# State-space input projection: two weight units that split the contraction instead of the columns, 192 matmuls of 512 moving columns for 384 of 256

## The chip, the cores and the metric

The kernel runs on 1 core of one Trainium2 chip. The metric is the device time of the whole kernel in microseconds (us). TensorE (PE) multiplies, VectorE (DVE), ScalarE (ACT) and GpSimd (POOL) work element by element, and SyncE (SP) issues most of the loads. PEld in the profile is TensorE's weight load, which is recorded apart from the matmul.

## The reference

One layer of a hybrid encoder on 1024 tokens of 1024 channels in float32. The part that matters here is the input projection and what becomes of its columns `u`:

```python
h = rmsnorm(x, g_mix_pre[l])
z = h @ w_in[l]                                   # 1024 x 1024 by 1024 x 4864
q, k, v, u, qx, gates = jnp.split(z, _IN_SPLITS, axis=-1)
y_attn = sliding_window_attention(q, k, v, sinks[l])
y_ssm = s5_branch(u, ...)                         # u: 1024 tokens x 512 columns
y_mem = memory_cross_attention(qx, km, vm)
gt = jax.nn.sigmoid(gates.reshape(B, L, N_BRANCH, D_MODEL))
merged = gt[:, :, 0] * (y_attn @ w_branch_attn[l]) + gt[:, :, 1] * (y_ssm @ w_branch_ssm[l]) + gt[:, :, 2] * (y_mem @ w_branch_mem[l])
x = x + rmsnorm(merged @ w_out[l], g_mix_post[l])
# then the MLP: x = x + rmsnorm(square(relu(rmsnorm(x) @ w_up)) @ w_down)
```

The change touches `u` = h times columns 768 to 1279 of `w_in`: 1024 tokens, a contraction of 1024, 512 columns out.

## The kernel before, in words

**Products.** Every large product is made in three matmuls for each 128 rows of the contraction. A float32 operand is split into a rounded part (`hi`) and the rest (`lo`), both of type fp32r, and `product` (L1345) adds hi*hi, hi*lo and lo*hi in a PSUM bank. The first operand of `matmul` after the bank is the stationary one, which a weight load (LDWEIGHTS) puts into the array, and the second is the moving one. Both may be 128 partitions; the moving one has up to 512 columns here. In the rows of the profile, `bank<-whi,hThi` names the moving operand first and the stationary one second.

**Weight units.** The weights come in units of 128 partitions by 2048 elements (1 MB), in two slots of `raw`, `whi` and `wlo`; unit `u` uses slot `u % 2`. For each unit SP issues two DMAs into `raw` (`load`, L293), ACT makes `whi` from it (`prep_hi`, L279), DVE makes `wlo` (`prep_lo`, L285), and TensorE waits for `wlo` (`unit`, L1354). `load` of unit u waits until DVE has made `wlo` of unit u-2. `prep_hi` of unit u waits, through the bank that its last argument names, until TensorE has finished with unit u-2. The units around the change are 9 (gate piece 0), 10 and 11 (`U_U`, the projection of u), 12 (gate piece 1) and 13 (gate piece 2).

**Order.** Each engine has its own order written out by hand, with semaphores between them. The results in PSUM are numbered events; event n uses bank n % 8. TensorE waits with `wait_free` until the bank's event n-8 was taken, and the engine that takes event n waits with `wait_full`. TensorE's order around the change is: gate piece 0 (`g0`, 4 events), scores of the sliding-window attention (`ssc`, 16 events, L1483), projection of u (`u`, 8 events), gate piece 1 (`g1`, 4 events), transposes and products of the attention (`spv`, L1364 and L1524), gate piece 2, and then the state-space layer.

**Projection of u.** `hThi` and `hTlo` hold the normalised input with channels in partitions, 128 channels by 1024 tokens for each of 8 values of k. The state-space layer wants tokens grouped by their number modulo 8, so the stationary operand is a view of `hThi` with step 8: the 128 tokens t = 8c + i for one i, whose elements lie 32 bytes apart in each partition (L1488, `STEP` = 8). Everywhere else in the kernel the stationary operand is contiguous. The moving operand is 256 columns of the weights, so a unit holds all 8 values of k for half of the columns. Two values of i share a bank.

**Other engines meanwhile.** DVE normalises the 16 score tiles (`s_normalise`, L1052 to L1062) while TensorE is in the projection; in DVE's order this stands between `prep_lo` of unit 11 and `prep_lo` of unit 12, and `prep_lo` of unit 13 follows. ACT takes the eight events of u (`copy_out`, L519) and writes them to `uc`, a view of `tok`, for the state-space layer.

Of the kernel before, what the change touches and what calls it, by code (L numbers as in the profile page):

```python
# [19 lines left out]
KT = D // P  # L20
# [5 lines left out]
W512 = 512  # L26
BT = W512 // P
# [3 lines left out]
STEP = 8  # L31
NC8 = L // STEP
NPAIR = 16
SG = 16
ST = 64
RP = 4
C_V, C_U, C_QX, C_G = 640, 768, 1280, 1792
# [3 lines left out]
U_MEM, U_QX, U_Q, U_KV, U_U, U_MERGE_A, U_GLU, U_MERGE_M, U_MERGE_S, U_OUT, U_MLP = 0, 4, 6, 8, 10, 23, 25, 27, 29, 31, 35  # L41
# [9 lines left out]
FIRST = {}  # L51
# [45 lines left out]
def hybrid_layer(nc, a, out):  # L97
# [4 lines left out]
    with ctx:  # L102
# [97 lines left out]
        uc = tok[:, :].rearrange("p (g i c) -> p g i c", g=32, i=STEP)  # L200
# [9 lines left out]
        banks = [ctx.enter_context(nc.psum_tensor(f"bank{b}", [P, 512], f32)) for b in range(8)]  # L210
        bank_full = [sem(f"bank_full{b}") for b in range(8)]
# [40 lines left out]
        def wait_free(eng, n, it=0, per=0):  # L252

            if n >= 8:
                eng.wait_ge(bank_free[n % 8], n // 8 + it * (per // 8))
# [17 lines left out]
        def prep_hi(act, u, n_before, it=0, per=0, ev=0):  # L273

            dmas = 2 * (u // 2 + 1) + (2 if u >= U_Q else 0)
            act.wait_ge(w_loaded[u % 2], 16 * dmas + it * (16 * per))
            if n_before is not None:
                wait_full(act, n_before, it, ev)
            nc.scalar.activation(parts(u)[0], raw[:, u % 2, :], ACT.Copy).then_inc(w_hi, 1)  # L279
# [7 lines left out]
        def wviews(u, kt):  # L287
            w = UNIT // kt
            return (whi[:, u % 2, :].rearrange("p (k c) -> p k c", c=w), wlo[:, u % 2, :].rearrange("p (k c) -> p k c", c=w))


        @block.sync
        def _(sp):  # L293
            def load(u, pieces, it=0, per=0):

                if u >= 2:
                    sp.wait_ge(w_lo, u - 1 + it * per)
                for dst, src in pieces:
                    sp.dma_start(dst, src).then_inc(w_loaded[u % 2], 16)

            def cols(u, src, kt=KT):

                v = raw[:, u % 2, :].rearrange("p (k c) -> p k c", k=kt)
                s = src.rearrange("(k p) c -> p k c", p=P)
                h = kt // 2
                return [(v[:, 0:h, :], s[:, 0:h, :]), (v[:, h:kt, :], s[:, h:kt, :])]

            for idx in range(2):
                sp.dma_start(xst[:, idx, :], a["mem"][0][idx * P:(idx + 1) * P, :]).then_inc(mem_in[idx], 16)
            sp.dma_start(gmem[:, :], a["g_mem"][0].partition_broadcast(P)).then_inc(gains_in, 16)  # L310
            w_in = a["w_in"][0]
            for s in range(4):
                load(U_MEM + s, cols(U_MEM + s, a["w_mem_kv"][0][:, s * 256:(s + 1) * 256]))
            for s in range(2):
                load(U_QX + s, cols(U_QX + s, w_in[:, C_QX + s * 256:C_QX + (s + 1) * 256]))
            for s in range(2):

                u = U_Q + s
                v = raw[:, u % 2, :].rearrange("p (k i j c) -> p k i j c", k=KT, i=2, j=2)
                src = w_in[:, 0:512].rearrange("(k p) (j i c) -> p k i j c", p=P, j=2, c=HD)  # L320
                load(u, [(v[:, :, i, j, :], src[:, :, 2 * s + i, j, :]) for i in range(2) for j in range(2)])
            load(U_KV, cols(U_KV, w_in[:, 512:768]))
            gate = lambda i: load(U_GATE[i], cols(U_GATE[i], w_in[:, C_G + 256 * i:C_G + 256 * (i + 1)]))
            gate(0)
            for s in range(2):
                load(U_U + s, cols(U_U + s, w_in[:, C_U + s * 256:C_U + (s + 1) * 256]))
            for i in range(1, 12):
                gate(i)
            for s in range(2):
                u = U_MERGE_A + s  # L330
                v = raw[:, u % 2, :].rearrange("p (k c) -> p k c", k=BT)
                load(u, [(v[64 * j:64 * j + 64, :, :], a["w_branch_attn"][0][256 * j:256 * j + 256, s * 512:s * 512 + 512]
                          .rearrange("(k p) c -> p k c", p=HD)) for j in range(2)])
            for s in range(2):
                u = U_GLU + s
                v = raw[:, u % 2, :].rearrange("p (k h c) -> p k h c", k=BT, h=2)
                src = a["w_glu"][0].rearrange("(k p) (h c) -> p k h c", p=P, h=2)
                load(u, [(v[:, :, h, :], src[:, :, h, s * 256:(s + 1) * 256]) for h in range(2)])
            for first, name in ((U_MERGE_M, "w_branch_mem"), (U_MERGE_S, "w_branch_ssm")):
                for s in range(2):  # L340
                    load(first + s, cols(first + s, a[name][0][:, s * 512:s * 512 + 512], BT))
            for s, c in enumerate((1, 0, 2, 3)):
                load(U_OUT + s, cols(U_OUT + s, a["w_out"][0][:, c * 256:(c + 1) * 256]))
            up, down = a["w_up"][0], a["w_down"][0]
            with sp.Fori(0, 8) as it:
                for s in range(2):
                    load(U_MLP + s, cols(U_MLP + s, up[:, bass.ds(it * 512 + s * 256, 256)]), it, 4)
                for s in range(2):
                    load(U_MLP + 2 + s, cols(U_MLP + 2 + s, down[bass.ds(it * 512, 512), s * 512:(s + 1) * 512], BT), it, 4)
            for t in range(NT):  # L350
                sp.wait_ge(out_made, t + 1)
                sp.dma_start(out[0, t * P:(t + 1) * P, :], tok[:, (1 + t % 3) * D:(2 + t % 3) * D]).then_inc(out_sent[t % 3], 16)
            for s, count in enumerate((3, 3, 2)):
                sp.wait_ge(out_sent[s], 16 * count)
# [158 lines left out]
        def _(act):  # L513
            A = nc.scalar

            def copy_out(n, dst, src=None):

                wait_full(act, n)
                A.activation(dst, banks[n % 8][:, :] if src is None else src, ACT.Copy).then_inc(bank_free[n % 8], 1)  # L519
# [32 lines left out]
            for s in range(4):  # L552
                n0 = FIRST["front"] + 4 + 6 * s
# [14 lines left out]
            n = FIRST["spar"]  # L568
            copy_out(n, spar[:, :, :].rearrange("p a b -> p (a b)"), banks[n % 8][:, 0:48])

            for s in range(2):
                n0 = FIRST["qx"] + 4 * s
# [18 lines left out]
            for s in range(2):  # L591
                n0 = FIRST["q"] + 4 * s
                prep_hi(act, U_Q + s + 1, n0 - 1)
                for i in range(2):
                    for half in range(2):
                        n = n0 + 2 * i + half
                        copy_out(n, qwin[:, s, i, 8 * half:8 * half + 8, :], banks[n % 8][:, :].rearrange("p (n c) -> p n c", c=CH))
            n0 = FIRST["kv"]
# [35 lines left out]
                    A.activation(prob[:, e, :], prob[:, e, :], ACT.Exp).then_inc(s_exp, 1)  # L634
            A.activation(sinkx[:, :, :], sinkx[:, :, :], ACT.Exp).then_inc(sink_exp, 1)

            for s in range(2):
                n0 = FIRST["u"] + 4 * s
                prep_hi(act, U_U + s + 1, n0 - 1)
                for jj in range(4):  # L640
                    n = n0 + jj
                    src = banks[n % 8][:, :].rearrange("p (j g c) -> p j g c", j=2, c=SG)
                    copy_out(n, uc[:, 16 * s:16 * s + 16, 2 * jj:2 * jj + 2, :].rearrange("p g j c -> p j g c"), src)
            gates(1)

            for q in range(8):
                for nn in range(2):
                    n = FIRST["spv"] + pv_event(q, nn)
# [4 lines left out]
            for ri in range(2):  # L653
                n = FIRST["spc"] + ri
                wait_full(act, n)
                src = banks[n % 8][:, :].rearrange("p (k g o) -> p g k o", g=2, o=SG)
                A.activation(cpk[0:64, ri, :, :], src[0:64, 0, :, :], ACT.Copy)
                A.activation(cpk[64:P, ri, :, :], src[64:P, 1, :, :], ACT.Copy).then_inc(bank_free[n % 8], 1)
            for r in range(4):
                n0 = FIRST[f"s5a{r}"]  # L660
# [5 lines left out]
                for e in range(2):  # L666
                    n = FIRST[f"s5m{r}"] + e
# [25 lines left out]
            for e in range(8):  # L693
                n = FIRST["yg"] + e
# [647 lines left out]
        def _(pe):  # L1342
            T = nc.tensor

            def product(dst, lhs, rhs, kt, start=True, stop=True, ready=None):  # L1345

                for k in range(kt):
                    if ready:
                        ready(k)
                    for i, (p, q) in enumerate(((0, 0), (0, 1), (1, 0))):  # L1350
                        ins = T.matmul(dst, lhs(k)[p], rhs(k)[q], start=start and k == 0 and i == 0,  # L1351
                                       stop=stop and k == kt - 1 and i == 2)
                return ins
# [121 lines left out]
            for e in range(16):  # L1475
                n = FIRST["ssc"] + e
                j = e % 2
# [10 lines left out]
            for s in range(2):  # L1488
                u = U_U + s
                unit(u)  # L1490
                hi, lo = wviews(u, KT)
                for jj in range(4):
                    n = FIRST["u"] + 4 * s + jj
                    wait_free(pe, n)
                    for ii in range(2):
                        i = 2 * jj + ii
                        ins = product(banks[n % 8][:, ii * 256:ii * 256 + 256], lambda k: (hs[0][:, k, i, :], hs[1][:, k, i, :]),
                                      lambda k: (hi[:, k, :], lo[:, k, :]), KT)
                    ins.then_inc(bank_full[n % 8], 1)
            gates(1)  # L1500

            pe.wait_ge(s_prob, 16)
# [228 lines left out]
```

## Time and profile before

| what | value |
|---|---|
| time, median of 3 runs | 1685.59 us (1683.85 to 1686.29) |
| span of the profiled execution, first to last instruction | 1684.2 us |
| PE busy | 1626.0 us, 97% of the span |
| DVE busy | 835.1 us, 50% |
| ACT busy | 431.4 us, 26% |
| POOL busy | 120.0 us, 7% |
| mean granted TensorE clock | 0.987 |

No device time of the profiled execution stands beside its span, so the span is what the profile gives for it. It lies inside the range of the three runs and 1.4 us below their median. Busy shares are averages over stages with different limits, and a busy PE can be a PE whose matmuls are spaced out: the start-to-start distance of neighbouring matmuls in the timeline tells how fast they really go.

### The profile page before, as it was taken

The page shows a single profiled execution, that of the slowest core. Times are in us where ns is not written, and L with a number is a line of the kernel's source. Part 1 is how long each engine was busy: PE and PEld are TensorE (multiplying, and loading weights), DVE is VectorE, ACT ScalarE, POOL GpSimd, SP SyncE. Part 2 cuts the span into 40 slices and gives each one's busy share as a digit, 9 for nine tenths or more (in the row PEclk, how much of TensorE's full clock was granted, in tenths as well). Part 3 has the DMA queues.
Part 4 walks back from the last instruction along what each step waited for, and adds up shares of the span by engine and source line. Part 5 has one row for each costly group of instructions (what it writes and reads, how often), then busy time and mean ns, then how long its engine had stood idle before and what let it go on. Part 6 is the DMA issues. An engine that isn't in the chain of part 4 may idle for free.

```text
span 1684.2 us, 18730 instructions
## 1 busy us (share of the span) xinstructions
PE 1626.0 (97%) x7615; PEld 1358.1 (81%) x7615; DVE 835.1 (50%) x1590; ACT 431.4 (26%) x588; POOL 120.0 (7%) x193
## 2 busy tenths in 40 slices
PE   4899999999999999999999999999999999999997
PEld 4788769997888888888888778888888888888885
DVE  5839458404854672545667643333333333333348
ACT  4333213013312223421133330212121211212131
POOL 2000000003221122100100200000000000000000
PEclk9899998999999999999999989999999999999999
DMA  7401110014122224533442321111111011111104
GB/s 259 104 25 51 57 63 32 25 38 132 60 76 72 88 63 134 192 105 105 146 145 88 119 94 50 50 51 50 50 50 50 25 50 50 50 50 50 50 0 162
DMA packets 83089, 130.96 MB, mean 78 GB/s; under 512 B 13104, under 2 KB 57168, under 8 KB 83024
## 3 DMA queue, kind: packets, MB, share of 16 engines
q1 hardware_dynamic: 67280, 76.03, 14.2%
q0 software_dynamic: 15744, 54.03, 9.6%
q8 instruction: 45, 0.74, 0.2%
q14 instruction: 20, 0.16, 0.0%
HBM read 104.88 MB, written 25.17 MB: 77 GB/s over the span
## 4 chain that ended last, share of the span: by engine, by line
PE 90%; DVE 6%; DMA 2%; ACT 1%; issue 1%; SPq 0%; DVEq 0%; ACTq 0%
PE bank L1351 84%; DMA raw<-in_w_mem_kv_dram 2%; PE bank L1364 2%; PE bank L1568 1%; PE bank L1456 1%; PE bank L1582 1%; DVE tok L1321 1%; DVE wlo L285 1%; DVE yst L1313 1%; PE bank L1524 0%; DVE acc L1328 0%; PE bank L1483 0%; PE bank L1551 0%; PE bank L1586 0%; DVE prob L946 0%
## 5 line engine op out<-in xcount | busy, mean ns | idle before, releaser
L1351 PE MATMUL bank<-hThi,whi 128*128 128x512 f32 x1184 | 465.4, 393 | 4.2 <-DVE hTlo L1263 1.6
L1351 PE MATMUL bank<-hTlo,whi 128*128 128x512 f32 x1184 | 463.8, 392 | 0.0
L1351 PE MATMUL bank<-hThi,wlo 128*128 128x512 f32 x1184 | 463.4, 391 | 0.0
L1351 PEld LDWEIGHTS bank<-hThi,whi 128*128 128x128 f32 x1184 | 224.1, 189 | 52.8 <-issue 6.3
L1351 PEld LDWEIGHTS bank<-hThi,wlo 128*128 128x128 f32 x1184 | 224.1, 189 | 47.3
L1351 PEld LDWEIGHTS bank<-hTlo,whi 128*128 128x128 f32 x1184 | 224.1, 189 | 46.3
L285 DVE TENSOR_TENSOR wlo<-raw,whi 128x2048 fp32r<-128x2048 f32 x65 | 148.9, 2291 | 138.5 <-ACT whi L279 138.3
L279 ACT ACTIVATE whi<-raw 128x2048 fp32r<-128x2048 f32 x65 | 124.2, 1910 | 357.7 <-PE bank L1351 327.2
L1351 PE MATMUL bank<-whi,yhi 128*128 128x512 f32 x512 | 202.6, 396 | 0.6 <-DVE wlo L285 0.6
L1351 PE MATMUL bank<-wlo,yhi 128*128 128x512 f32 x512 | 202.5, 396 | 0.0
L1351 PE MATMUL bank<-whi,ylo 128*128 128x512 f32 x512 | 202.5, 395 | 0.0
L1304 DVE TENSOR_TENSOR acc<-bank,acc 128x512 f32<-128x512 f32 x112 | 76.7, 690 | 175.2 <-PE bank L1351 175.2
L1289 DVE TENSOR_TENSOR yst<-scr 128x512 f32<-128x512 f32 x64 | 44.3, 692 | 168.8 <-ACT scr L780 168.8
L1351 PEld LDWEIGHTS bank<-whi,yhi 128*128 128x128 f32 x512 | 96.3, 188 | 24.2 <-DVE wlo L285 1.0
L1351 PEld LDWEIGHTS bank<-wlo,yhi 128*128 128x128 f32 x512 | 96.3, 188 | 23.2
L1351 PEld LDWEIGHTS bank<-whi,ylo 128*128 128x128 f32 x512 | 96.3, 188 | 23.1
L780 ACT ACTIVATE scr<-bank 128x512 f32<-128x512 f32 x64 | 38.3, 598 | 198.2 <-PE bank L1351 198.2
L1351 PE MATMUL bank<-whi,hThi 128*128 128x256 f32 (+1 forms) x208 | 80.6, 387 | 1.1 <-DVE hTlo L1214 1.1
L1351 PE MATMUL bank<-whi,hTlo 128*128 128x256 f32 (+1 forms) x208 | 79.8, 383 | 0.0
L1351 PE MATMUL bank<-wlo,hThi 128*128 128x256 f32 (+1 forms) x208 | 79.7, 383 | 0.0
L623 ACT ACTIVATE scr<-bank 128x512 f32<-128x512 f32 x48 | 28.6, 598 | 185.1 <-PE bank L1351 182.1
L1291 DVE TENSOR_TENSOR ylo<-yst,yhi 128x512 fp32r<-128x512 f32 x64 | 44.4, 693 | 44.7 <-ACT yhi L782 44.7
(306 smaller groups left out, 1858.8 us busy)
## 6 DMA issues: line engine op xcount, KB each, us to landing
raw<-in_w_in_dram SPq DMA_DIRECT2D x34, 512.0 KB, 4.7
raw<-in_w_up_dram SPq DMA_DIRECT2D x32, 512.0 KB, 4.4
raw<-in_w_down_dram SPq DMA_DIRECT2D x32, 512.0 KB, 4.4
gate_scratch<-scr POOLq DMA_DIRECT2D x48, 256.0 KB, 2.3
tok<-gate_scratch POOLq DMA_DIRECT2D x24, 512.0 KB, 3.6
raw<-in_w_mem_kv_dram SPq DMA_DIRECT2D x8, 512.0 KB, 11.1
y_scratch<-yst POOLq DMA_DIRECT2D x16, 256.0 KB, 2.7
yst<-y_scratch POOLq DMA_DIRECT2D x16, 256.0 KB, 5.2
```

The lines of the kernel that those rows point to most:

```text
L279: nc.scalar.activation(parts(u)[0], raw[:, u % 2, :], ACT.Copy).then_inc(w_hi, 1)
L285: nc.vector.tensor_tensor(lo, raw[:, u % 2, :], hi.bitcast(f32), sub).then_inc(w_lo, 1)
L623: A.activation(scr[:, gp % 2, :], banks[n % 8][:, :], ACT.Sigmoid).then_inc(bank_free[n % 8], 1)
L780: A.activation(scr[:, pc % 2, :], banks[n % 8][:, :], ACT.Relu).then_inc(bank_free[n % 8], 1)
L1289: V.tensor_tensor(yst[:, pc % 4, :], scr[:, pc % 2, :], scr[:, pc % 2, :], mul).then_inc(f_sq, 1)
L1291: V.tensor_tensor(ylo[:, ct, h], yst[:, pc % 4, :], yhi[:, ct, h].bitcast(f32), sub).then_inc(f_lo, 1)
L1304: V.tensor_tensor(acc[:, t, h], banks[n % 8][:, :], acc[:, t, h], add).then_inc(bank_free[n % 8], 1)
L1313: mark(V.tensor_tensor(yx[:, t % 2, :], acc[:, t, :], tok[:, 0:D], mul))
L1321: V.scalar_tensor_tensor(out=xt, in0=yx[:, t % 2, :], scalar=stat[:, 1:2], in1=xt, op0=mul, op1=add).then_inc(out_made, 1)
L1351: ins = T.matmul(dst, lhs(k)[p], rhs(k)[q], start=start and k == 0 and i == 0, stop=stop and k == kt - 1 and i == 2)
L1364: ins = T.transpose(banks[n % 8][:, i * P:i * P + P] if dsts is None else dsts[i], src, ident[:, :])
L1456: ins = T.matmul(banks[n % 8][:, :], vm[:, m, h * P:h * P + P], pT[:, q % 2, m, :], start=m == 0, stop=m == 1)
```

## The change

Each of the two units now holds all 512 columns for half of the contraction: 4 values of k by 512 columns. TensorE goes twice over the 8 values of i, with 4 values of k each time. In the first pass it opens the eight banks, one for each i; in the second it adds to them and marks each bank full. So there are 2 x 8 x 4 x 3 = 192 matmuls with 512 moving columns for 2 x 8 x 8 x 3 = 384 with 256. Each bank is now one value of i with all 512 columns, and ACT copies it in one piece. On ACT, `prep_hi` of unit 12 now comes ahead of all eight copies, and waits for the first bank of the second pass.

```diff
@@ SP: loads
             for s in range(2):
-                load(U_U + s, cols(U_U + s, w_in[:, C_U + s * 256:C_U + (s + 1) * 256]))
+                load(U_U + s, cols(U_U + s, w_in[512 * s:512 * s + 512, C_U:C_U + W512], BT))
@@ ACT
-            for s in range(2):
-                n0 = FIRST["u"] + 4 * s
-                prep_hi(act, U_U + s + 1, n0 - 1)
-                for jj in range(4):
-                    n = n0 + jj
-                    src = banks[n % 8][:, :].rearrange("p (j g c) -> p j g c", j=2, c=SG)
-                    copy_out(n, uc[:, 16 * s:16 * s + 16, 2 * jj:2 * jj + 2, :].rearrange("p g j c -> p j g c"), src)
+            n0 = FIRST["u"]
+            for s in range(2):
+                prep_hi(act, U_U + s + 1, n0 - 1 + s)
+            for i in range(STEP):
+                copy_out(n0 + i, uc[:, :, i, :], banks[(n0 + i) % 8][:, :].rearrange("p (g c) -> p g c", c=SG))
@@ TensorE
-                hi, lo = wviews(u, KT)
-                for jj in range(4):
-                    n = FIRST["u"] + 4 * s + jj
-                    wait_free(pe, n)
-                    for ii in range(2):
-                        i = 2 * jj + ii
-                        ins = product(banks[n % 8][:, ii * 256:ii * 256 + 256], lambda k: (hs[0][:, k, i, :], hs[1][:, k, i, :]),
-                                      lambda k: (hi[:, k, :], lo[:, k, :]), KT)
-                    ins.then_inc(bank_full[n % 8], 1)
+                hi, lo = wviews(u, BT)
+                for i in range(STEP):
+                    n = FIRST["u"] + i
+                    if s == 0:
+                        wait_free(pe, n)
+                    ins = product(banks[n % 8][:, :], lambda k: (hs[0][:, BT * s + k, i, :], hs[1][:, BT * s + k, i, :]),
+                                  lambda k: (hi[:, k, :], lo[:, k, :]), BT, start=s == 0, stop=s == 1)
+                    if s:
+                        ins.then_inc(bank_full[n % 8], 1)
```

TensorE's order where the projection of u begins, before (the first bank of u is bank 3; it goes on in this bank for 48 matmuls):

```order
L1483 MATMUL bank1<-kT,tok 128x128 x4
L1483 MATMUL bank2<-kT,tok 128x128 x4
L1351 MATMUL bank3<-whi,hThi 128x256
L1351 MATMUL bank3<-wlo,hThi 128x256
L1351 MATMUL bank3<-whi,hTlo 128x256
```

And of the change, around the end of bank 3 in the first pass (the change's L1349 is L1351 of before):

```order
L1349 MATMUL bank3<-whi,hThi 128x512
L1349 MATMUL bank3<-wlo,hThi 128x512
L1349 MATMUL bank3<-whi,hTlo 128x512
L1349 MATMUL bank4<-whi,hThi 128x512
L1349 MATMUL bank4<-wlo,hThi 128x512
```

The moving operand is twice as wide, the stationary ones are the same views with step 8, and the bank changes after 12 matmuls.

ACT's order from the last exponential of the scores on, before (`tok` is where `uc` lies; the three rows with `whi` are units 11, 12 and 13):

```order
L635 ACTIVATE sinkx<-sinkx 128x64
L279 ACTIVATE whi<-raw 128x2048
L519 ACTIVATE tok<-bank 128x2x16x16 x4
L279 ACTIVATE whi<-raw 128x2048
L519 ACTIVATE tok<-bank 128x2x16x16 x4
L279 ACTIVATE whi<-raw 128x2048
L623 ACT_TABLE_LOAD
```

And of the change:

```order
L635 ACTIVATE sinkx<-sinkx 128x64
L279 ACTIVATE whi<-raw 128x2048 x2
L519 ACTIVATE tok<-bank 128x32x16 x8
L279 ACTIVATE whi<-raw 128x2048
L623 ACT_TABLE_LOAD
```

The rounding of unit 12 moved ahead of the copies; DVE's order does not change.

## Rows read from the trace of the kernel before

**Rows 1.** The page: span, busy time of the engines, chain by engine and line.

```profile
span 1684.2 us, 18730 instructions
...
PE 1626.0 (97%) x7615; PEld 1358.1 (81%) x7615; DVE 835.1 (50%) x1590; ACT 431.4 (26%) x588; POOL 120.0 (7%) x193
...
PE 90%; DVE 6%; DMA 2%; ACT 1%; issue 1%; SPq 0%; DVEq 0%; ACTq 0%
```

**Rows 2.** Waits of PE, 225 to 700 us, the largest: in total, times, longest.

```profile
PE bank L1551 <- ACT wT L519: 5.0, 4, 1.9
```

**Rows 3.** Windows: the projection of u in two stretches, then gate piece 1.

```profile
core 0: us, PE busy (x) PEld busy (x) DVE busy (x) ACT busy (x) POOL busy (x), PEclk, DMA share, GB/s
...
268.90:271.95 3.05, 3.05 (x14) 3.05 (x13) 2.91 (x9) 1.13 (x3) 0.00 (x0) 0.50 0.00 0
271.95:361.63 89.68, 89.68 (x373) 89.68 (x372) 37.72 (x90) 11.37 (x16) 0.00 (x0) 1.00 0.07 24
361.63:383.50 21.87, 21.87 (x98) 18.08 (x98) 2.29 (x1) 5.48 (x6) 1.62 (x3) 1.00 0.27 85
```

**Rows 4.** Timeline, PE, projection of u: start, us, instruction; then gate piece 1.

```profile
268.90 0.61 PE L1351 MATMUL bank<-whi,hThi 128*128 128x256 f32 x1
269.31 0.44 PE L1351 MATMUL bank<-wlo,hThi 128*128 128x256 f32 x1
...
271.71 0.41 PE L1351 MATMUL bank<-whi,hTlo 128*128 128x256 f32 x1
...
272.38 0.40 PE L1351 MATMUL bank<-whi,hTlo 128*128 128x256 f32 x1
...
361.28 0.40 PE L1351 MATMUL bank<-wlo,hThi 128*128 128x256 f32 x1
...
361.76 0.39 PE L1351 MATMUL bank<-hThi,whi 128*128 128x512 f32 x1
```

**Rows 5.** Groups of weight loads in the projection of u, then in gate piece 1.

```profile
L1351 PEld LDWEIGHTS bank<-wlo,hThi 128*128 128x128 f32 x128 | 43.3, 338 | 0.0
...
L1351 PEld LDWEIGHTS bank<-hTlo,whi 128*128 128x128 f32 x32 | 6.0, 188 | 1.2
```

**Rows 6.** Timeline, PE, gate piece 0: 512 columns, contiguous stationary operand.

```profile
229.20 0.63 PE L1351 MATMUL bank<-hThi,wlo 128*128 128x512 f32 x1
...
233.90 0.63 PE L1351 MATMUL bank<-hTlo,whi 128*128 128x512 f32 x1
...
235.06 0.40 PE L1351 MATMUL bank<-hThi,wlo 128*128 128x512 f32 x1
...
252.77 0.39 PE L1351 MATMUL bank<-hThi,wlo 128*128 128x512 f32 x1
```

**Rows 7.** Timeline, PE, memory projection: 256 columns, contiguous stationary operand.

```profile
36.09 0.28 PE L1351 MATMUL bank<-mThi,whi 128*128 128x256 f32 x1
...
40.91 0.28 PE L1351 MATMUL bank<-mThi,wlo 128*128 128x256 f32 x1
```

**Rows 8.** Timeline, DVE: last scores read, then `wlo` of units 11 and 12.

```profile
267.75 0.69 DVE L1046 SCALAR_TENSOR_TENSOR prob<-bank,mx 128x512 f32<-128x512 f32 x1
...
278.89 0.69 DVE L1046 SCALAR_TENSOR_TENSOR prob<-bank,mx 128x512 f32<-128x512 f32 x1
...
282.36 2.29 DVE L285 TENSOR_TENSOR wlo<-raw,whi 128x2048 fp32r<-128x2048 f32 x1 [2.72 <-ACT whi L279]
...
311.40 0.69 DVE L1062 TENSOR_TENSOR prob<-prob,den 128x512 f32<-128x512 f32 x1
318.02 2.29 DVE L285 TENSOR_TENSOR wlo<-raw,whi 128x2048 fp32r<-128x2048 f32 x1 [5.93 <-ACT whi L279]
```

**Rows 9.** Timeline, ACT: `whi` of unit 12.

```profile
316.09 1.90 ACT L279 ACTIVATE whi<-raw 128x2048 fp32r<-128x2048 f32 x1
```

**Rows 10.** Timeline, PE: matmuls of plain float32 with 512 columns, two records each.

```profile
210.59 3.60 PE L1456 MATMUL bank<-pT,vm 128*128 128x512 f32 x8
```

**Rows 11.** The page: DMA issues of the input weights, median us to landing.

```profile
raw<-in_w_in_dram SPq DMA_DIRECT2D x34, 512.0 KB, 4.7
```

## The prediction

> **What bounds the kernel now.** First I read the page. PE is busy 97% of the span, and the chain that ended last is 90% PE [rows 1]. A busy share does not say how fast the matmuls go, so next I took the windows of the stage that changes. The projection of u lies between 268.90 and 361.63 us, where PE has no idle time, while DVE works 40.6 us and ACT 12.5 us [rows 3]. From its first matmul to the first of gate piece 1 it takes 361.76 - 268.90 = 92.86 us [rows 4]. The waits of PE in the middle of the kernel are small, 5.0 us for the largest in 475 us [rows 2]: TensorE sets the pace there, and what the stage loses or gains moves everything behind it.
>
> Then the timeline, for the distance from start to start. In the projection of u, 368 steps between 272.38 and 361.28 give 88.90 / 368 = 241.6 ns for a matmul with 256 moving columns [rows 4]. In gate piece 0, with 512 moving columns, 78 steps between 235.06 and 252.77 give 17.71 / 78 = 227.1 ns [rows 6]. So half as many columns take longer here. With 256 columns and a contiguous stationary operand, 41 steps from 36.09 to 40.91 give 4.82 / 41 = 117.6 ns [rows 7]. What is different about u is the stationary view with step 8: its weight load is recorded with 338 ns, the contiguous one of gate piece 1 with 188 [rows 5]. The stage runs at the pace of its weight loads: 384 x 241.6 = 92.8 us.
>
> The first 3 us tell how load and stream combine. From 268.90 to 271.95 the granted clock is 0.50, which is the 1.2 GHz level [rows 3]. There 10 steps from 269.31 to 271.71 give 240 ns [rows 4], as at full clock. At that level 512 columns take 427 ns, (233.90 - 229.20) / 11 [rows 6], so an estimate for the stream of 256 is 213 ns. If load and stream stood one behind the other, the load would have had 27 ns. So they lie beside each other, and the distance is the longer of the two.
>
> The Trainium skill, "SBUF — State Buffer", section "Door 1: The DMA port swizzle", says that SBUF is read in 16-byte lines and that each element from a new line costs more; elements 32 bytes apart are in lines of their own. The longer load in the trace agrees.
>
> **The change part by part.**
>
> *The matmuls.* There are 192 for 384. The views with step 8 stay, so each keeps its slow load, and 192 loads fall away. No row shows such a load beside 512 moving columns at full clock. Below, the bound is 227.1 ns, the stream of 512 columns with fast loads [rows 6]. Above, it is load and stream in full succession: the load would be 241.6 less half of the 256-column stream at 1.2 GHz, 241.6 - 107 = 135 ns, and with 213 ns of stream that makes 348 ns. I take 241.6. The nearest row is the low-clock one: a stream of 213 ns, as long as 512 columns take at full clock, was wholly covered by the same load.
>
> The Trainium skill, "TensorE: Matmul & The Clock Gate", section "The mechanism" of part 3, says against this that a weight load overlaps with matmuls in flight only when it goes to other row groups; here every load fills all rows. By that rule the distance is the 348 ns of the upper bound, and the gain shrinks to 25 us. The low-clock rows speak against it.
>
> *The start.* The clock is low until 271.95, and I leave that instant where it is, since PE has the same work before it and is busy in either case. The start costs 0.41 us for the first step against 0.24, so 0.17 extra [rows 4]. From 269.07 on, 7 matmuls at 427 ns [rows 6] take 2.99 us, to 272.06. The other 185 take 185 x 0.2416 = 44.70 us, to 316.76. There gate piece 1 has its first matmul, where it had it at 361.76 [rows 4]: **45.0 us** earlier.
>
> *The second unit.* Pass 2 begins at 272.06 + 89 x 0.2416 = 293.6 and needs `wlo` of unit 11, made at 282.36 + 2.29 = 284.65 [rows 8]. It has 8.9 us to spare. Its DMAs are of the same size (median 4.7 us to landing) [rows 11], and were long done.
>
> *The banks.* Pass 1 needs a new bank each 2.9 us (5.1 at low clock) and DVE frees them every 1.6 us, the last at 278.89 + 0.69 = 279.58 [rows 8]: (278.89 - 267.75) / 7 = 1.59. The eighth is wanted at about 293.6 - 2.9 = 290.7. No wait. Adding to a bank in pass 2 is what every matmul after the first of a product does already; I put nothing for it.
>
> *The unit behind.* Gate piece 1 needs `wlo` of unit 12 at 316.76. ACT rounds it after the first bank of pass 2, at 293.6 + 2.9 = 296.5, plus 1.9 [rows 9], so 298.4. DVE has 16 score tiles in its order first, ending at 311.40 + 0.69 = 312.09 with hardly a gap between them, then takes 2.29 us: 314.4 [rows 8]. So 2.4 us are to spare, where before it had 361.76 - 320.31 = 41. This is the new near miss: if the stage took 227.1 ns for each matmul it would end at 272.06 + 185 x 0.2271 = 314.1, and PE would wait for DVE until 314.4. The earliest start of gate piece 1 is 314.4 whatever the matmuls do, a gain of at most 47.4 us.
>
> *ACT.* Eight copies of 0.6 us in 23 us instead of in 93; each has 2.9 us. The first begins behind the rounding of unit 12, at 298.4 rather than 296.5, and is done before the third bank is full. The gates want bank 3 again only after 316.76. Hidden; without that cover the eight copies would cost 4.8 us. The DMAs with longer rows (2 KB for 1 KB) are hidden behind the same slack as before.
>
> *Behind the stage.* ACT, DVE and POOL have nothing in the old stage that was waiting for a later time: their orders go on with gate piece 1 and move with it. DVE's long idle time before unit 13 was a wait for TensorE's last matmul of u. So nothing should give the 45 us back.
>
> The sum: the profiled span 1684.2 - 45.0 = 1639.2. The span is 1.4 us under the median 1685.6; for the median the same subtraction gives **1640.6 us**.
>
> **The rivals.**
>
> *The loads slow the wide stream a little* (250 to 270 ns). For it: at full clock the moving operand is read twice as fast as at low clock, beside a load that already has trouble reading, and even contiguous loads leave 227.1 rather than 213. Against it: 240 against 241.6 ns at the two clocks, so the doubled read rate cost 1.6 ns. At 255 ns: 185 x 13.4 ns = 2.5 us lost, 1643.1; at 270, 1645.9.
>
> *Load and stream one after the other* (348 ns). For it: nothing in the trace but that the case is not seen at full clock. Against it: the 213 ns stream inside 240 ns. 185 x 0.348 = 64.4 us, end at 336.4, gain 25.3, time 1660.3. I give it 4%.
>
> *The step 8 is not what holds, and the wide matmuls go at 227 ns.* Then DVE's unit 12 decides, at 314.4: 1685.6 - 47.4 = 1638.2. For it: the distance of 241.6 was only measured with 256 columns. Against it: then 256 columns would have needed less than 241.6. 8%.
>
> *Slower than before.* The wide matmul with this load would have to take over 92.86 / 192 = 484 ns. The mechanism would be the pace of the plain float32 matmuls, 3.60 us for four matmuls or 0.90 us each [rows 10], if a strided fp32r operand forced the array into it with 512 columns: 192 x 0.90 = 173 us, 80 more, 1765.6. Gate piece 0 runs fp32r at 512 columns in one record of 227 ns [rows 6], and u has the same type. 1%. No change at all would need just 484 ns: also 1%.
>
> **How the numbers follow.** A difference under 0.2% (3.4 us) can't be told from no change in this kernel. The forecast of 241.6 ns, up to 249, has 71%, the mild slowing 15%, succession 4%, DVE's bound 8%, and the two last 1% each. So faster has 98%, same 1%, slower 1%. The low end is the DVE bound less the 1.7 us by which the lowest run lay under the median, rounded: 1637. The high end takes in the mild slowing to 270 ns and the same spread upward, 1648. Outside it lie succession and the two last, and tails of the others.
>
> **What the new profile would show.** Distance from start to start in the u stage about 0.24 us, with 512 columns and loads of some 338 ns; wrong if 0.227, 0.25 or more, or 0.35. Gate piece 1 begins near 316.7. PE waits for `wlo` of L285 at that place not at all, or for under a microsecond. DVE's score tiles end near 312.1 as before. The copies of ACT come each 2.9 us. All later stages have the old lengths; if the sum of the kernel falls by less than the stage does, a later wait took it back, and the list of PE's waits names it. A clock that falls to the low level at another place, or rises later than 271.95 here, would move the time by some 0.4 us for each microsecond at it in this stage.

## The result and the profile after

The changed kernel takes 1641.03 us (median of 4 runs, 1640.36 to 1642.88); beside it the kernel before took 1685.94 us (4 runs, 1683.85 to 1686.52). The ratio is 0.974, 95% interval 0.9726 to 0.9753. That is 44.9 us less between the medians. The two profiled spans differ by a little less, 1684.2 - 1640.7 = 43.5 us. The profiled execution of the changed kernel took 1642.88 us, the longest of the four; the spans of the other three were 1638.2, 1638.6 and 1639.0 us.

The page of the changed kernel: span, busy time, chain by engine and by line.

```profile
span 1640.7 us, 18345 instructions
...
PE 1580.5 (96%) x7423; PEld 1311.9 (80%) x7423; DVE 834.7 (51%) x1590; ACT 431.3 (26%) x588; POOL 120.0 (7%) x193
...
PE 90%; DVE 6%; DMA 2%; ACT 1%; issue 1%; SPq 0%; DVEq 0%; ACTq 0%
```

TensorE lost 45.5 us of busy time and 192 matmuls; the other engines work as long as before, and the chain has the same shares as in [rows 1]. The windows of the changed kernel, over the projection of u at low and at full clock, and over gate piece 1, answer to [rows 3]:

```profile
core 0: us, PE busy (x) PEld busy (x) DVE busy (x) ACT busy (x) POOL busy (x), PEclk, DMA share, GB/s
268.42:273.18 4.76, 4.76 (x12) 3.89 (x12) 4.55 (x13) 1.87 (x4) 0.00 (x0) 0.50 0.00 0
273.18:317.63 44.45, 44.45 (x182) 44.37 (x182) 35.99 (x86) 10.75 (x15) 0.00 (x0) 1.00 0.14 43
317.63:339.50 21.87, 21.87 (x98) 17.99 (x97) 2.29 (x1) 5.47 (x6) 1.62 (x3) 1.00 0.28 94
```

The stage lasts 49.21 us for 92.86, which is 43.65 less, and gate piece 1 is as long as before, 21.87 us. The timeline of PE in the changed kernel (start, duration, instruction) gives the distance, as [rows 4] did:

```profile
268.42 0.82 PE L1349 MATMUL bank<-whi,hThi 128*128 128x512 f32 x1
269.04 0.63 PE L1349 MATMUL bank<-wlo,hThi 128*128 128x512 f32 x1
...
273.26 0.40 PE L1349 MATMUL bank<-whi,hTlo 128*128 128x512 f32 x1
...
274.22 0.41 PE L1349 MATMUL bank<-whi,hThi 128*128 128x512 f32 x1
...
316.91 0.40 PE L1349 MATMUL bank<-whi,hThi 128*128 128x512 f32 x1
...
317.63 0.40 PE L1349 MATMUL bank<-hThi,whi 128*128 128x512 f32 x1
```

At full clock 174 steps take 316.91 - 274.22 = 42.69 us, or 245.3 ns each. At low clock there are 11 matmuls, from 268.42 to 273.26. The waits of PE in the changed kernel between 225 and 660 us, the first three of the list:

```profile
PE bank L1549 <- ACT wT L519: 5.0, 4, 1.9
PE bank L1362 <- DVEq L1024: 1.9, 2, 1.3
PE bank L1349 <- issue: 1.4, 1, 1.4
```

The largest is the old one of [rows 2], and none is for the `wlo` of L285. No new wait of PE shows there. Gate piece 1 begins 44.1 us earlier than before (317.63 for 361.76) and the span is 43.5 us shorter, so what follows took 0.6 us more; no row says where, and it is within the scatter of the spans.

### The profile page after: what moved, and what is told of

Its sections match the earlier page's. It is cut to its first block, busy times and chain, and to the rows that moved or that the text cites. A ratio compares the mean times of both kernels' runs of the same rounds, so it can differ in the third digit from the quotient of the medians.

```text
span 1640.7 us, 18345 instructions
## 1 busy us (share of the span) xinstructions
PE 1580.5 (96%) x7423; PEld 1311.9 (80%) x7423; DVE 834.7 (51%) x1590; ACT 431.3 (26%) x588; POOL 120.0 (7%) x193
## 4 chain that ended last, share of the span: by engine, by line
PE 90%; DVE 6%; DMA 2%; ACT 1%; issue 1%; SPq 0%; DVEq 0%; ACTq 0%
PE bank L1349 83%; DMA raw<-in_w_mem_kv_dram 2%; PE bank L1362 2%; PE bank L1566 1%; PE bank L1454 1%; PE bank L1580 1%; DVE tok L1319 1%; DVE wlo L285 1%; DVE yst L1311 1%; PE bank L1522 0%; DVE acc L1326 0%; PE bank L1549 0%; PE bank L1584 0%; PE bank L1481 0%; DVE prob L944 0%
## 5 line engine op out<-in xcount | busy, mean ns | idle before, releaser
L1349 PE MATMUL bank<-hThi,whi 128*128 128x512 f32 x1184 | 464.7, 393 | 4.4 <-DVE hTlo L1261 1.8
L1349 PE MATMUL bank<-hTlo,whi 128*128 128x512 f32 x1184 | 463.1, 391 | 0.0
L1349 PE MATMUL bank<-hThi,wlo 128*128 128x512 f32 x1184 | 463.1, 391 | 0.0
L1349 PEld LDWEIGHTS bank<-hThi,whi 128*128 128x128 f32 x1184 | 224.0, 189 | 52.5 <-issue 4.3
L1349 PEld LDWEIGHTS bank<-hThi,wlo 128*128 128x128 f32 x1184 | 223.7, 189 | 47.1
L1349 PEld LDWEIGHTS bank<-hTlo,whi 128*128 128x128 f32 x1184 | 223.8, 189 | 46.3
L1349 PE MATMUL bank<-whi,yhi 128*128 128x512 f32 x512 | 202.6, 396 | 0.6 <-DVE wlo L285 0.6
L1349 PE MATMUL bank<-wlo,yhi 128*128 128x512 f32 x512 | 202.5, 395 | 0.0
L1349 PE MATMUL bank<-whi,ylo 128*128 128x512 f32 x512 | 202.5, 395 | 0.0
L285 DVE TENSOR_TENSOR wlo<-raw,whi 128x2048 fp32r<-128x2048 f32 x65 | 148.9, 2291 | 94.9 <-ACT whi L279 94.8
L1349 PEld LDWEIGHTS bank<-whi,yhi 128*128 128x128 f32 x512 | 96.3, 188 | 24.1 <-DVE wlo L285 1.1
L1349 PEld LDWEIGHTS bank<-wlo,yhi 128*128 128x128 f32 x512 | 96.3, 188 | 23.2
L1349 PEld LDWEIGHTS bank<-whi,ylo 128*128 128x128 f32 x512 | 96.3, 188 | 23.2
L1349 PE MATMUL bank<-whi,hThi 128*128 128x512 f32 (+1 forms) x144 | 55.7, 387 | 1.1 <-DVE hTlo L1212 1.1
L503 POOL DMA_DIRECT2D tok<-x_scratch x8 | 4.2, 529 | 696.9 <-DMA out_dram<-tok 690.3
L1349 PE MATMUL bank<-wlo,hThi 128*128 128x512 f32 (+1 forms) x144 | 54.6, 379 | 0.0
```

The costliest lines, as they stand in the source:

```text
L285: nc.vector.tensor_tensor(lo, raw[:, u % 2, :], hi.bitcast(f32), sub).then_inc(w_lo, 1)
```

## The experiments

The theory was that in this stage a matmul's distance is the longer of its weight load and its stream of moving columns, and that the load is slow because the stationary view has step 8. Against it stood: the two come one after the other; a matmul has a fixed cost here whatever its operands; and the split of the contraction, with its bank order, gains by itself. The ratios below are to the kernel before, run on the same chip.

**The kernel before with a contiguous stationary view** (`narrow_contig`). The tokens of u come out in another order, so the output is not the reference's. In the diffs here and below, lines that are not shown are those of the kernel named.

```diff
-            hs = [h[:, :, :].rearrange("p k (c i) -> p k i c", i=STEP) for h in (hThi, hTlo)]
+            hs = [h[:, :, :].rearrange("p k (i c) -> p k i c", i=STEP) for h in (hThi, hTlo)]
```

> The kernel before with one edit: the stationary view of the projection of u takes 128 neighbouring tokens instead of every eighth, so u comes out with its tokens in another order. The 384 matmuls of 256 columns stay. Theory (the weight load with step 8 sets the pace): the distance falls from 241.6 ns to the 117.6 ns of the memory projection, the stage to about 268.5 + 4.8 us at low clock (22 matmuls) + 362 x 0.1176 = 315.9, so it gains about 46 us and reaches 1640. Rival (a matmul has a fixed cost of some 240 ns here, whatever its stationary operand, and the change gains by having fewer of them): no change, 1686.

Measured: 1640.09 us (1638.02 to 1643.52), ratio 0.9736 (0.972 to 0.9752). The timeline of PE in this run:

```profile
274.01 0.28 PE L1351 MATMUL bank<-whi,hThi 128*128 128x256 f32 x1
...
311.93 0.28 PE L1351 MATMUL bank<-wlo,hThi 128*128 128x256 f32 x1
...
315.77 0.40 PE L1351 MATMUL bank<-hThi,whi 128*128 128x512 f32 x1
```

316 steps in 37.92 us are 120.0 ns each, half of the 241.6 with step 8, and gate piece 1 begins at 315.77. All 384 matmuls are there and the whole gain too: their number was not the cost, and a fixed cost per matmul is out. Taking away the step and halving the number of loads are two ways to nearly the same place.

**The changed kernel with the same contiguous view** (`wide_contig`).

> The changed kernel with the contiguous stationary view (tokens of u in another order). Theory: the 245 ns of the changed kernel fall to 227, the stage ends near 314.3, just before or at the 314.0 at which DVE has made the low part of unit 12: 1638, that is 3 us under the changed kernel and 48 under the one before. Rival (fixed cost per matmul): 1641, as the changed kernel.

Measured: 1640.37 us (1636.35 to 1641.04), ratio 0.9728 (0.9712 to 0.9744). The timeline of PE:

```profile
275.07 0.39 PE L1349 MATMUL bank<-whi,hThi 128*128 128x512 f32 x1
...
311.81 0.39 PE L1349 MATMUL bank<-whi,hThi 128*128 128x512 f32 x1
```

162 steps in 36.74 us, 226.8 ns each: as in gate piece 0 [rows 6]. The distance falls as expected. The expected 3 us less in the whole kernel is as large as the scatter of its runs, and the intervals of the two ratios overlap, so the total does not show it.

**Half the width again** (`narrow_128`): the kernel before with 768 matmuls of 128 columns.

```diff
-                        ins = product(banks[n % 8][:, ii * 256:ii * 256 + 256], lambda k: (hs[0][:, k, i, :], hs[1][:, k, i, :]),
-                                      lambda k: (hi[:, k, :], lo[:, k, :]), KT)
+                        for h in range(2):
+                            ins = product(banks[n % 8][:, ii * 256 + h * P:ii * 256 + h * P + P], lambda k: (hs[0][:, k, i, :], hs[1][:, k, i, :]),
+                                          lambda k: (hi[:, k, h * P:h * P + P], lo[:, k, h * P:h * P + P]), KT)
```

> The kernel before with each matmul of 256 moving columns of the projection of u made as two of 128, each with its own load of step 8: 768 for 384. Theory (the longer of load and stream): 240 ns each whatever the width, the stage doubles, 1686 + 93 = 1779. Rival (load and stream one after the other, 135 + 53 = 188 ns): 768 x 0.188 = 144 us, 1686 + 52 = 1738.

Measured: 1777.03 us (1775.97 to 1778.61), ratio 1.0547 (1.053 to 1.0565). The stage runs from 265.98 to 450.35 us here, 184.4 us. A window over all but its first 2 us, and its weight loads as a group over the same window:

```profile
268.00:450.00 182.00, 182.00 (x760) 182.00 (x759) 38.75 (x92) 11.73 (x16) 0.00 (x0) 0.50 0.04 12
```

```profile
L1351 PEld LDWEIGHTS bank<-whi,hThi 128*128 128x128 f32 x253 | 85.3, 337 | 0.0
```

760 matmuls in 182.00 us, about 240 ns each, with half the columns: the stage doubles, and the kernel is 92 us slower. The recorded length of a load, 337 ns, is longer than that distance: the records of neighbouring loads overlap, and it is the distance that gives the pace. The granted clock is 0.50 in the whole window, the 1.2 GHz level. The kernel before had 240 ns too at this level, with 256 columns [rows 4]. At that level 128 columns are about 107 ns of stream and 256 about 213, both estimates from the 427 of 512 columns [rows 6]. A sum of load and stream would differ by 107 ns between the two; measured are 240 and 240. So they lie beside each other. The Trainium skill says in "TensorE: Matmul & The Clock Gate", section "The mechanism" of part 3, that a weight load overlaps with matmuls in flight only when the row groups differ. These loads all fill the whole array, and the 240 ns at both widths speak against that sentence. The prediction passed over that this section of the Trainium skill also lets a load into the background weight buffer go ahead of matmuls in flight, which the 240 ns agree with.

The low clock was not free. Behind the stage, the first matmuls of gate piece 1 still go at its level:

```profile
452.16 0.63 PE L1351 MATMUL bank<-hTlo,whi 128*128 128x512 f32 x1
...
454.72 0.53 PE L1351 MATMUL bank<-hTlo,whi 128*128 128x512 f32 x1
455.09 0.39 PE L1351 MATMUL bank<-hThi,wlo 128*128 128x512 f32 x1
```

Six steps in 2.56 us are 427 ns each. From 450.35 to 455.09 eleven steps take 4.74 us where 2.50 would do, 2.2 us more.

**The two passes with narrow matmuls** (`split_narrow`): the changed kernel with two matmuls of 256 columns for each of 512. The passes are closed groups, so the first half of the contraction is left out of u.

```diff
-                    ins = product(banks[n % 8][:, :], lambda k: (hs[0][:, BT * s + k, i, :], hs[1][:, BT * s + k, i, :]),
-                                  lambda k: (hi[:, k, :], lo[:, k, :]), BT, start=s == 0, stop=s == 1)
+                    for h in range(2):
+                        c = slice(h * 256, h * 256 + 256)
+                        ins = product(banks[n % 8][:, c], lambda k: (hs[0][:, BT * s + k, i, :], hs[1][:, BT * s + k, i, :]),
+                                      lambda k: (hi[:, k, c], lo[:, k, c]), BT)
```

> The changed kernel with its two passes, its bank order and ACT's new order, but each wide matmul made as two of 256 columns. The passes are closed groups, so the sum over the first half of the contraction is left out of u. Theory: splitting the contraction by itself gives nothing, only the halved number of loads does; 384 x 241.6 ns as before, 1686. Rival (the bank order, or not sharing a bank between two token groups, is what gains): between 1641 and 1686, for example 1663 if it is half.

Measured: 1684.88 us (1683.57 to 1686.46), ratio 1.0002 (0.9993 to 1.0012). Its timeline of PE:

```profile
276.01 0.41 PE L1349 MATMUL bank<-wlo,hThi 128*128 128x256 f32 x1
...
359.99 0.40 PE L1349 MATMUL bank<-whi,hTlo 128*128 128x256 f32 x1
```

349 steps in 83.98 us are 240.6 ns. New loads, new passes, new bank order, ACT's new order, and nothing gained. By itself the split of the contraction gains nothing; it is what makes room for 512 columns in a unit of the same size.

**ACT's order undone** (`wide_prep_late`), in the changed kernel:

```diff
-            for s in range(2):
-                prep_hi(act, U_U + s + 1, n0 - 1 + s)
+            prep_hi(act, U_U + 1, n0 - 1)
             for i in range(STEP):
                 copy_out(n0 + i, uc[:, :, i, :], banks[(n0 + i) % 8][:, :].rearrange("p (g c) -> p g c", c=SG))
+            prep_hi(act, U_U + 2, n0)
```

> The changed kernel with one part of the change undone: ACT rounds unit 12 behind its eight copies of u, not ahead of them. Theory (the short stage needs this order): ACT ends the last copy at 318.4, rounds until 320.3, DVE makes the low part until 322.6, and TensorE, done with u at 317.6, waits 5.0 us; if its clock falls in that wait, another 1 to 3 us. So 1646 to 1649. Rival (the order on ACT is without effect, since DVE's share comes late anyway): 1641.

Measured: 1649.72 us (1646.04 to 1650.0), ratio 0.978 (0.9764 to 0.9797), some 9 us above the changed kernel by their medians and just over the 1649 expected. Its timeline of all engines where u ends:

```profile
317.96 0.40 PE L1349 MATMUL bank<-whi,hTlo 128*128 128x512 f32 x1
318.39 0.60 ACT L519 ACTIVATE tok<-bank 128x512 f32<-128x512 f32 x1 [2.35 <-PE bank L1349]
318.89 3.70 ACT L279 ACTIVATE whi<-raw 128x2048 fp32r<-128x2048 f32 x2
320.82 4.49 DVE L285 TENSOR_TENSOR wlo<-raw,whi 128x2048 fp32r<-128x2048 f32 x2 [7.83 <-ACT whi L279]
...
323.17 0.80 PE L1349 MATMUL bank<-hThi,whi 128*128 128x512 f32 x1 [4.81 <-DVE wlo L285]
```

ACT rounds units 12 and 13 after its last copy, DVE makes the low part of unit 12 from 320.82 on, and TensorE starts 5.0 us after the 318.2 at which it would have. After the wait the clock is at the 1.2 GHz level (the window from 323.17 to 329.00 us, which takes in the rise, has a mean of 0.63). The rows behind the wait, in the timeline of PE, show the distance of 427 ns and then of 230:

```profile
325.89 0.63 PE L1349 MATMUL bank<-hThi,whi 128*128 128x512 f32 x1
326.32 0.63 PE L1349 MATMUL bank<-hTlo,whi 128*128 128x512 f32 x1
...
327.54 0.39 PE L1349 MATMUL bank<-hTlo,whi 128*128 128x512 f32 x1
327.77 0.40 PE L1349 MATMUL bank<-hThi,wlo 128*128 128x512 f32 x1
```

Ten matmuls from 323.17 to 327.54 take 4.37 us where 2.27 would do: 2.1 us on top. The two make 7.1 us. The spans differ by as much, 1647.8 - 1640.7, but spans of one kernel scatter by 2 us and more, so the match is no closer than that. This one moved line on ACT keeps about a sixth of the gain.

**Steps 2 and 4 in the kernel before** (`narrow_step2`, `narrow_step4`). The tokens of u come out in other orders. With step 2:

```diff
-            hs = [h[:, :, :].rearrange("p k (c i) -> p k i c", i=STEP) for h in (hThi, hTlo)]
+            hs = [h[:, :, :].rearrange("p k (b c i) -> p k b i c", c=P, i=2) for h in (hThi, hTlo)]
...
-                        ins = product(banks[n % 8][:, ii * 256:ii * 256 + 256], lambda k: (hs[0][:, k, i, :], hs[1][:, k, i, :]),
+                        ins = product(banks[n % 8][:, ii * 256:ii * 256 + 256], lambda k: (hs[0][:, k, i // 2, i % 2, :], hs[1][:, k, i // 2, i % 2, :]),
```

> The kernel before, 384 matmuls of 256 columns, with a stationary view of step 2 (every second token, elements 8 bytes apart; u comes out in another token order). Theory by 16-byte lines: two elements still share a line, so the load is not the limit or little slower, 120 to 125 ns, 1640. Rival (the cost grows with the number of bytes skipped, or any step but 1 is slow): 240 ns, 1685, or half way, 1660.

> The same with step 4, elements 16 bytes apart. Theory by 16-byte lines: every element has a line of its own, as with step 8, so 240 ns and 1685. Rival (the cost grows in proportion to the step): some 180 ns, 1662.

Measured: step 2 1641.28 us (1640.25 to 1643.25), ratio 0.9741 (0.9725 to 0.9758); step 4 1680.76 us (1680.01 to 1682.73), ratio 0.9972 (0.996 to 0.9983). The weight loads of each as a group between 274 and 312 us, step 2 first:

```profile
L1351 PEld LDWEIGHTS bank<-whi,hThi 128*128 128x128 f32 x106 | 20.7, 195 | 0.0
```

```profile
L1351 PEld LDWEIGHTS bank<-wlo,hThi 128*128 128x128 f32 x55 | 18.1, 329 | 0.0
```

The timeline of PE with step 2:

```profile
276.04 0.28 PE L1351 MATMUL bank<-whi,hTlo 128*128 128x256 f32 x1
...
311.92 0.28 PE L1351 MATMUL bank<-wlo,hThi 128*128 128x256 f32 x1
```

And with step 4:

```profile
276.10 0.40 PE L1351 MATMUL bank<-wlo,hThi 128*128 128x256 f32 x1
...
354.97 0.40 PE L1351 MATMUL bank<-whi,hThi 128*128 128x256 f32 x1
```

Step 2 is as fast as contiguous, 299 steps in 35.88 us or 120.0 ns; step 4 costs 78.87 us / 338 = 233.3 ns, nearly all that step 8 costs. The jump lies between elements 8 and 16 bytes apart. The Trainium skill, "SBUF — State Buffer", section "Door 1: The DMA port swizzle", says that SBUF has lines of 16 bytes and that a read wants at least two elements of each. That agrees with where the jump lies. The same note of the Trainium skill then gives 4 values of fp32 as how far one can stride for free; if a step of 4 is meant, the 233.3 ns are against it. The runs show the place of the jump, not that lines are its cause. The step from 4 to 8 costs another 8 ns, which the line alone does not explain; over 384 matmuls it is 3.2 us and most of the 4.6 by which `narrow_step4` beat the kernel before.

**Steps 4 and 2 in the changed kernel** (`wide_step4`, `wide_step2`), one run each, with the same edit of the view.

> The changed kernel with the stationary view at step 4 (u in another token order). With 256 columns step 4 gave 233.3 ns and step 8 241.6; the changed kernel has 245.3. If the wide stream makes each slow load some 4 ns longer (theory), the distance here is 237. If 245 is not made by the load but is a cost of the wide matmul with any slow load (rival), it stays at 245.

> The same at step 2. With 256 columns step 2 went at 120.0 ns, as fast as contiguous. Theory: the stream of 512 columns is the longer of the two, 227 ns. Rival (any strided load disturbs the wide stream): 230 to 245.

Measured: 1641.24 and 1640.03 us. The timelines of PE, step 4 first:

```profile
276.12 0.40 PE L1349 MATMUL bank<-whi,hThi 128*128 128x512 f32 x1
...
311.84 0.40 PE L1349 MATMUL bank<-whi,hTlo 128*128 128x512 f32 x1
```

```profile
276.07 0.39 PE L1349 MATMUL bank<-wlo,hThi 128*128 128x512 f32 x1
...
312.00 0.39 PE L1349 MATMUL bank<-whi,hTlo 128*128 128x512 f32 x1
```

Step 4: 152 steps in 35.72 us, 235.0 ns. Step 2: 154 steps in 35.93 us, 233.3 ns. With step 4 the distance follows the load and does not stay at 245, so the rival is out; but the wide stream adds 1.7 ns and not the 4 of the theory. With step 2 it is the theory that missed, with 227, and the rival's 230 to 245 that came: the load is hidden with narrow matmuls, and yet the wide ones take 6.5 ns more than with a contiguous view. Each distance rests on one profiled execution.

The distances in one table (full clock; 128 columns at low clock):

| step of the stationary view | 128 columns | 256 columns | 512 columns |
|---|---|---|---|
| 1 | | 120.0 ns | 226.8 ns |
| 2 | | 120.0 ns | 233.3 ns |
| 4 | | 233.3 ns | 235.0 ns |
| 8 | 240 ns | 241.6 ns | 245.3 ns |

## Why the prediction was right

**The mechanism** was right in each of its steps. That the slow load sets the pace: `narrow_contig` takes it away and gains all. That load and stream lie beside each other: `narrow_128` for widths below, the changed kernel itself for 512 columns at full clock, 245.3 ns and not 348. (The prediction calls 213 ns as long as 512 columns take at full clock. That is half of 427; the row for it is 227.1 [rows 6], still under 241.6.) That 192 loads fall away and the rest of the edit is neutral: `split_narrow`.

**The term of the matmuls** was 185 x 241.6 ns; it came out as 181 at 245.3. The first rival, a mild slowing, is real and worth 181 x 3.7 ns = 0.7 us. It is much smaller than the 250 to 270 ns at which I priced it.

**The term of the clock** was 7 matmuls at low clock, with the rise left at 271.95. It was 11: in the profiled execution of the change the stage began at 268.42 and the clock rose at 273.18. The four more cost 4 x (427 - 242) = 0.7 us. The two terms are, within 0.1 us, the difference between the 47.86 us worked out for the stage and the 49.21 measured. In the other runs of this study the clock rose at other places near here (275 us in `wide_contig`, with u starting at 270.03). The time of its rise was not something to carry over from one trace.

**The banks and the second unit** were as worked out; PE has no wait in the stage. **The unit behind**: this is DVE's `wlo` of unit 12 in the changed kernel, in its place behind the last score tile, and it follows without a wait:

```profile
310.93 0.69 DVE L1060 TENSOR_TENSOR prob<-prob,den 128x512 f32<-128x512 f32 x1
311.54 2.29 DVE L285 TENSOR_TENSOR wlo<-raw,whi 128x2048 fp32r<-128x2048 f32 x1
```

So it was ready at 313.83 and TensorE wanted it at 317.63: 3.8 us to spare, for 2.4 worked out, because the stage ended later and DVE began 0.5 us earlier. `wide_prep_late` shows that this margin hangs on the moved line of ACT.

**The rivals.** Succession and the slow float32 pace did not come. DVE as the bound did not either, but it was near where the loads are fast. In `wide_contig`, at 226.8 ns, gate piece 1 began at 315.89 without a wait for DVE, whose `wlo` of unit 12 was ready only 0.4 us earlier, at 313.18 + 2.29 = 315.47.

The 1640.6 predicted for the median stands against 1641.03. That they are so near is partly luck. Both sized terms erred by 0.7 us in the same direction, read from the slowest of the four executions; and the medians moved by 1.4 us more than the profiled spans did, which made up for it. The span worked out, 1639.2, was missed by 1.5 us in the profiled execution (1640.7) and lies just above the other three.

**What stays open.** Why a wide stream adds 1.7 to 6.5 ns beside a strided load, most where the load is fastest, and why step 8 costs 8 ns more than step 4. And no version here beats the change and computes the same thing: the contiguous view, which would give 181 x 18.5 ns = 3.3 us, needs the tokens of `hThi` and `hTlo` in another order than the rest of the kernel reads them, or copies of both. I tried neither.

## What to carry to other kernels

Compare the start-to-start distance of a stage's matmuls with that of another stage of the same type before believing a busy share. Where fewer moving columns take as long or longer, look at the weight load: with elements 16 or 32 bytes apart it set a pace of 233 to 242 ns, about twice the 120.0 of a contiguous view with 256 columns. It is paid once for each matmul, so a contiguous view takes it away, and the widest moving operand hides nearly all of it (245.3 ns against 226.8). When a stage is shortened by half, go through each engine's order for the next stage's inputs: what had 41 us to spare had 3.8 left, and one line in the wrong place on ACT cost about 7.

## What the runs showed of the hardware

- A weight load of 128 x 128 fp32r with the elements 4 or 8 bytes apart keeps up with 120.0 ns for each matmul; with 16 bytes apart the distance is 233.3 ns, with 32 bytes 241.6 (`narrow_contig`, `narrow_step2`, `narrow_step4`, the kernel before).
- A load of the whole array lies beside the stream of the matmul before it: at 1.2 GHz 128 and 256 columns both go at 240 ns with step 8, and at 2.4 GHz 512 columns go at 245.3 ns.
- With step 8 the distance hardly depends on the clock of TensorE: 240 ns at 1.2 GHz and 241.6 at 2.4 GHz, both with 256 columns.
- In `narrow_128` the granted clock was 0.50, the 1.2 GHz level, through 182 us in which PE shows no gap. No cost of it shows in that stage, whose 240 ns are no more than the 241.6 of step 8 at full clock (128 columns at full clock were not run); it cost 2.2 us in gate piece 1 behind it.
- In `wide_prep_late` TensorE came from full clock (1.00 from 316.00 to 318.20), waited 5.0 us, and then took 4.37 us for ten matmuls of 512 columns, 2.1 us more than at full clock.
